# Ones multiplied until the first rows come, first weights split before the second turned pair, and other orders of the steps

## What is computed

```python
def first_block(x, p, ...):
    for i in range(DEPTH):                      # 2
        mix = mlstm_mixer(x, ...) if i < 1 else swa_sink_attention(x, ...)
        x = layer_norm(DEEPNORM_ALPHA * x + mix, mix_ln_g[i], mix_ln_b[i])
        x = layer_norm(DEEPNORM_ALPHA * x + squared_relu_mlp(x, ...), mlp_ln_g[i], mlp_ln_b[i])
        x = x + jax.nn.sigmoid(x @ ple_w_gate[i] + ple_b_gate[i]) * (p[i] @ ple_w_proj[i])
    return x

def second_block(x, p, ...):
    h = x + 0.5 * swiglu(rmsnorm(x, ffn1_norm), ...)
    u = rmsnorm(h, mix_norm) @ w_in
    h = h + mixed @ w_out                       # NSA (compressed, selected, window) and forgetting attention of u
    h = h + 0.5 * swiglu(rmsnorm(h, ffn2_norm), ...)
    gate = jax.nn.sigmoid(rmsnorm(h, ple_gate_norm) @ ple_w_gate)
    return h + gate * rmsnorm(p @ ple_w_proj, ple_norm)
```

## Time and profile before

| | us |
|---|---|
| median of 3 runs | 1218.65 |
| lowest and highest | 1217.24, 1219.37 |
| profiled execution, its time | 1217.5 |
| its span, first to last instruction | 1215.8 |
| TensorE busy | 1195.1 |
| VectorE busy | 744.2 |
| ScalarE busy | 619.4 |
| GpSimd busy | 42.6 |

### The profile page before, as it was taken

The page is one execution under the profiler, slowest core; times in us unless marked ns, Lnnn a source line. Parts: engine busy times, 40 slices in busy tenths (PEclk is TensorE's granted clock), DMA queues, the critical chain, the costliest instruction groups (busy, mean ns, idle before and its releaser), DMA issues.

```text
span 1215.8 us, 15115 instructions
## 1 busy us (share of the span) xinstructions
PE 1195.1 (98%) x5861; PEld 988.8 (81%) x5861; DVE 744.2 (61%) x983; ACT 619.4 (51%) x925; POOL 42.6 (4%) x61
## 2 busy tenths in 40 slices
PE   7999999999999999999999999999999999999998
PEld 6888788888778878888887888888878788888887
DVE  5759754556875675554596455547976465555446
ACT  5555444434465453443456344446886664444445
POOL 1000000000000000000001000001111010000000
PEclk9999999999999999999999999999999999999999
DMA  8555555555653456546555655554651336555550
GB/s 296 181 178 194 194 204 173 182 199 173 191 181 100 152 175 206 194 156 206 184 160 173 208 175 197 167 189 143 194 166 62 113 100 230 176 195 169 188 173 35
DMA packets 119959, 210.72 MB, mean 173 GB/s; under 512 B 8320, under 2 KB 67024, under 8 KB 119888
## 3 DMA queue, kind: packets, MB, share of 16 engines
q1 hardware_dynamic: 119344, 209.35, 52.2%
q10 hardware_dynamic: 544, 0.40, 0.1%
HBM read 208.68 MB, written 1.05 MB: 173 GB/s over the span
## 4 chain that ended last, share of the span: by engine, by line
PE 89%; DVE 7%; ACT 2%; issue 1%; POOL 0%; DMA 0%; DVEq 0%; ACTq 0%; POOLq 0%
PE psum L341 23%; PE psum L343 22%; PE psum L342 22%; PE psum L349 4%; PE psum L355 3%; PE psum L350 3%; PE psum L1364 2%; PE psum L1396 2%; PE psum L511 2%; DVE wl L324 2%; PE psum L1383 1%; PE psum L818 1%; PE psum L1370 0%; PE psum L1367 0%; ACT wh L314 0%
## 5 line engine op out<-in xcount | busy, mean ns | idle before, releaser
L293 DVE TENSOR_TENSOR wl<-ring,wh 128x2048 fp32r<-128x2048 f32 x131 | 300.0, 2292 | 269.2 <-ACT wh L284 269.0
L284 ACT ACTIVATE wh<-ring 128x2048 fp32r<-128x2048 f32 x131 | 250.7, 1916 | 219.1 <-PE psum L343 219.1
L341 PE MATMUL psum<-wh,xT_high 128*128 128x512 f32 (+4 forms) x816 | 319.8, 392 | 0.0
L343 PE MATMUL psum<-wh,xT_low 128*128 128x512 f32 (+4 forms) x816 | 312.7, 383 | 0.0
L342 PE MATMUL psum<-wl,xT_high 128*128 128x512 f32 (+4 forms) x816 | 312.0, 382 | 0.0
L341 PE MATMUL psum<-wh,hidT_high 128*128 128x512 f32 (+2 forms) x472 | 178.9, 380 | 0.2
L343 PEld LDWEIGHTS psum<-wh,xT_low 128*128 128x128 f32 x816 | 153.6, 188 | 30.0
L343 PE MATMUL psum<-wh,hidT_low 128*128 128x512 f32 (+2 forms) x472 | 177.9, 378 | 0.0
L342 PE MATMUL psum<-wl,hidT_high 128*128 128x512 f32 (+2 forms) x472 | 177.8, 378 | 0.0
L341 PEld LDWEIGHTS psum<-wh,xT_high 128*128 128x128 f32 x816 | 153.8, 188 | 28.7 <-issue 1.7
L342 PEld LDWEIGHTS psum<-wl,xT_high 128*128 128x128 f32 x816 | 153.9, 189 | 27.1
(11 more groups left out here) (301 smaller groups left out, 1311.2 us busy)
## 6 DMA issues: line engine op xcount, KB each, us to landing
ring<-in_mlp_w_up SPq DMA_DIRECT2D x32, 1024.0 KB, 5.3
ring<-in_mlp_w_down SPq DMA_DIRECT2D x32, 1024.0 KB, 4.9
ring<-in_ffn_wg SPq DMA_DIRECT2D x44, 512.0 KB, 4.0
ring<-in_ffn_wu SPq DMA_DIRECT2D x44, 512.0 KB, 5.0
ring<-in_ffn_wd SPq DMA_DIRECT2D x22, 1024.0 KB, 5.0
ring<-in_ple_w_gate SPq DMA_DIRECT2D x12, 1024.0 KB, 5.1
ring<-in_w_in SPq DMA_DIRECT2D x10, 1024.0 KB, 5.0
ring<-in_a_w_in SPq DMA_DIRECT2D x8, 1024.0 KB, 9.3
```

The source lines that it names most:

```text
L284: K.nc.scalar.activation(parts_of(K, n)[0][:, 0:w], K.ring[:, n % SLOTS, 0:w], ACT.Copy).then_inc(K.high_ready, 2)
L293: K.nc.vector.tensor_tensor(low[:, 0:w], K.ring[:, n % SLOTS, 0:w], high[:, 0:w].bitcast(F32), ALU.subtract).then_inc(K.low_ready, 2)
L341: nc.tensor.matmul(out, x[0], w[0], start=start, stop=False)
L343: return nc.tensor.matmul(out, x[1], w[0], start=False, stop=stop)
```

## The change

It has three parts.

1. VectorE sets the tile of ones first of all and signals it. TensorE waits for that signal and multiplies the tile with itself four times (float32, 128x256, into bank 0, which no one reads) ahead of its first step.
2. In the first stage's list "high 0, 0" and "low 0, 0" stand ahead of "xturn 1" for ScalarE and VectorE, and "high 0, 1" ahead of the first dense steps. Product 0's row tile 0 is done in pairs of k tiles: first high x high of both, as soon as the high weights are there, then low x high of both, then high x low, behind the wait for the low weights. The three products are the same, their order in the sum is not.
3. The lists of all tails and of the NSA stage have another order. No step is added or left out. The remaining 160 or so steps of the first stage's list keep their order.

The diff, cut: of part 3 it shows the list after the sinks, the one after the second embedding, and the stretch of the NSA list at the end of the dense work.

```diff
--- before.py
+++ after.py
@@ -925,27 +925,27 @@
     yield "stats", 0, 1
     yield "spread", 0
     yield "centre", 0, 0
+    yield "centre", 0, 1
     yield "normal", 0, 0
-    yield "centre", 0, 1
     yield "update", 1, 0
     yield "normal", 0, 1
+    yield "turn", 0, 0
     yield "last", 3, 1
-    yield "turn", 0, 0
     yield "turn", 0, 1
-    yield "high", 0, 0
+    yield "stats", 1, 0
+    yield "lead_low", 1, 0
     yield "update", 1, 1
     yield "low", 0, 0
-    yield "stats", 1, 0
     yield "stats", 1, 1
+    yield "lead_low", 1, 1
     yield "low", 0, 1
     yield "lead_high", 1, 0
     yield "lead_high", 1, 1
+    yield "high", 0, 0
     yield "high", 0, 1
     yield "lead", 0
     yield "lead", 1
-    yield "lead_low", 1, 0
     yield "spread", 1
-    yield "lead_low", 1, 1
     yield "centre", 1, 0
     yield "centre", 1, 1
     yield "normal", 1, 0
...
@@ -1112,15 +1112,17 @@
     yield "square", 0, 0
     yield "lead_high", 0, 1
     yield "lead_low", 0, 0
+    yield "gate", 0, 0
     yield "turn", 0, 0
-    yield "gate", 0, 0
+    yield "sigmoid", 0
     yield "lead_high", 1, 0
     yield "lead_high", 1, 1
     yield "high", 0, 0
-    yield "sigmoid", 0
     yield "high", 0, 1
+    yield "square", 0, 1
+    yield "sigmoid", 1
+    yield "logit", 0
     yield "lead_low", 0, 1
-    yield "logit", 0
     yield "gated", 0
     yield "gate", 0, 1
     yield "gate", 1, 0
@@ -1129,8 +1131,6 @@
     yield "lead_low", 1, 0
     yield "low", 0, 0
     yield "logit", 1
-    yield "sigmoid", 1
-    yield "square", 0, 1
     yield "low", 0, 1
     yield "gated", 1
     yield "lead_low", 1, 1
...
@@ -2152,343 +2152,343 @@
...
+        yield "take", 5, 0
+        yield "keep", 21
         yield "scores", 22
         yield "low", 18, 1
         yield "shares", 4
-        yield "take", 5, 0
         yield "high", 19, 0
+        yield "dense", 5, 1, 1, range(2)
+        yield "dense", 5, 1, 1, range(2, 4)
         yield "norm", 4
         yield "take", 5, 1
-        yield "dense", 5, 1, 1, range(2)
-        yield "keep", 21
-        yield "dense", 5, 1, 1, range(2, 4)
+        yield "turn", 20
+        yield "values", 19
+        yield "zturn", 0, 0
+        yield "high", 19, 1
+        yield "tiles", 4
+        yield "turn", 21
         yield "group", 4
-        yield "turn", 20
-        yield "zturn", 0, 0
-        yield "values", 19
-        yield "high", 19, 1
-        yield "turn", 21
-        yield "values", 20
-        yield "tiles", 4
         yield "low", 19, 0
-        yield "low", 19, 1
         yield "tiles", 5
         yield "tiles", 6
-        yield "values", 21
         yield "tiles", 7
         yield "scores", 23
+        yield "values", 20
+        yield "values", 21
         yield "keep", 22
         yield "turn", 22
-        yield "keep", 23
+        yield "low", 19, 1
         yield "scores", 24
         yield "out", 0, 0, 0
...
@@ -3027,12 +3027,12 @@
     def steps():
 
         yield "xturn", 0
-        yield "xturn", 1
         yield "high", 0, 0
         yield "low", 0, 0
+        yield "xturn", 1
+        yield "high", 0, 1
         yield "dense", 0, 0, 0, range(2)
         yield "dense", 0, 0, 1, range(2)
-        yield "high", 0, 1
         yield "low", 0, 1
         yield "xturn", 2
         yield "xturn", 3
@@ -3227,6 +3227,9 @@
 
     @block.tensor
     def _(pe):
+        pe.wait_ge(K.ones_ready, 1)
+        for i in range(4):
+            nc.tensor.matmul(K.psum[:, 0, 0:SEQ], K.ones[:, 0:P], K.ones[:, :], start=True, stop=True)
         for step, *args in steps():
             if step == "dense":
                 c, half, t, ks = args
@@ -3239,18 +3242,24 @@
                         pe.wait_ge((K.act_took if t == 0 else K.dve_took).sem, c - 1)
                 w = [joined(x, 4, width) for x in parts_of(K, n)]
                 out_c = K.psum[:, bank(c, t), 0:width]
+                if c == 0 and t == 0:
+                    xs = lambda k, part: K.xT[part][:, 4 * half + k, 0:P]
+                    for a in ks[::2]:
+                        pe.wait_ge(K.input_high.sem, (4 * half + a) // 2 + 1)
+                        pe.wait_ge(K.high_ready, 2 * n + 1 + a // 2)
+                        for k in (a, a + 1):
+                            nc.tensor.matmul(out_c, xs(k, 0), w[0][:, k, :], start=half == 0 and k == 0, stop=False)
+                        pe.wait_ge(K.input_low.sem, (4 * half + a) // 2 + 1)
+                        for k in (a, a + 1):
+                            nc.tensor.matmul(out_c, xs(k, 1), w[0][:, k, :], start=False, stop=False)
+                        weights_here(K, pe, n, a // 2)
+                        for k in (a, a + 1):
+                            mm = nc.tensor.matmul(out_c, xs(k, 0), w[1][:, k, :], start=False, stop=half == 1 and k == 3)
+                    if half == 1:
+                        mm.then_inc(K.filled.sem, 1)
+                    continue
                 for k in ks:
                     kk = 4 * half + k
-                    if c == 0 and t == 0:
-                        if k % 2 == 0:
-                            pe.wait_ge(K.input_high.sem, kk // 2 + 1)
-                            weights_here(K, pe, n, k // 2)
-                        product_high(K, out_c, stationary(K.xT)(kk, t), [x[:, k, :] for x in w], kk == 0)
-                        if k % 2 == 1:
-                            pe.wait_ge(K.input_low.sem, kk // 2 + 1)
-                            product_low(K, out_c, stationary(K.xT)(kk - 1, t), [x[:, k - 1, :] for x in w], False)
-                            mm = product_low(K, out_c, stationary(K.xT)(kk, t), [x[:, k, :] for x in w], kk == KT - 1)
-                        continue
                     if k % 2 == 0:
                         weights_here(K, pe, n, k // 2)
                     mm = product(K, K.psum[:, bank(c, t), 0:width], stationary(K.xT)(kk, t),
@@ -3468,10 +3477,11 @@
     def _(dve):
         ch = Chain(dve, K.dve_step)
         S, G = K.mstat, K.gates
+        nc.vector.memset(K.ones[:, :], 1.0).then_inc(K.ones_ready, 1)
         for ap, value in [(K.ident[:, :], 0.0), (K.sel[:, :, :], 0.0), (K.causal[:, :], 0.0),
                           (K.window[:, :], 0.0), (K.cmp_mask[:, :, :], 0.0), (K.cmp_keep[:, :, :], 1.0)]:
             nc.vector.memset(ap, value).then_inc(K.zeroed, 1)
-        for ap, value in [(K.ones[:, :], 1.0), (K.fox_bias[:, :], 0.0), (K.minus_half[:, :], -0.5),
+        for ap, value in [(K.fox_bias[:, :], 0.0), (K.minus_half[:, :], -0.5),
                           (K.v_ext[:, :, :, M_DV:M_DV + 1], 1.0), (K.cmp_v[:, :, :], 0.0),
                           (K.half_rows[0:HD, 0:1], 1.0), (K.half_rows[HD:P, 0:1], 0.0),
                           (K.half_rows[0:HD, 1:2], 0.0), (K.half_rows[HD:P, 1:2], 1.0)]:
@@ -4096,6 +4106,7 @@
         K.first_loaded = sem("first_loaded")
         K.small_loaded = sem("small_loaded")
         K.zeroed = sem("zeroed")
+        K.ones_ready = sem("ones_ready")
         K.masked = sem("masked")
         K.p_loaded = sem("p_loaded")
         K.stored = sem("stored")
```

More of the change, by code:

```diff
@@ L2269, in steps @@
-        yield "silu", 0
-        yield "dense", 3, 1, 0, range(2)
-        yield "high", 13, 1
-        yield "dense", 3, 1, 0, range(2, 4)
-        yield "gate", 2
-        yield "low", 13, 0
+        yield "keep", 4
+        yield "cw1", 1, 1, range(4, 8)
+        yield "high", 12, 0
+        yield "gate", 2
+        yield "high", 12, 1
+        yield "low", 12, 1
+        yield "high", 13, 0
+        yield "high", 13, 1
+        yield "turn", 4
+        yield "dense", 3, 1, 0, range(2)
+        yield "silu", 0
```

359 lines of the change are left out of this document (178 added, 181 removed).

## The result

The changed kernel took 1214.95 us (median of 7 executions, 1213.33 to 1215.91), the kernel before in the same rounds 1218.65 us. The ratio is 0.9969, with a 95% interval of 0.9959 to 0.998: 3.7 us faster, where 3.3 us were forecast. The profiled execution took 1214.99 us with a span of 1213.3 us, 2.5 us under the 1215.8 us of the profile before. So the two profiles show only part of what the medians show: the kernel before was profiled in an execution 1.15 us under its median, the changed one in an execution at its median. The gain read from rows (2.5 us) is not the gain of the medians (3.7 us).

The account below looks back on a forecast made before the run. TensorE is busy 98% of 1215.8 us, so gains lie in its 20 us of waits and slow-clock stretches. 2.4 + 0.6 + 0.3 = 3.3 us off the median of 1218.65 gave 1215.4 us, range 1212.8 to 1217.8.

Parts of the forecast that it names:

- The fillers and the splits: Start: high clock by the first dense matmul, up to 1.9 us; with earlier splits TensorE 4.2 us ahead after load 1.
- What is late next: Gate transposes: VectorE's copy of product 0, behind "bias", limits the start's lead to 2.4 us (bounds 1.9 to 2.8).
- The lists: Start: the small lists (gains, biases, positions) that "bias" waits for, forecast to land at 23.57 again.
- The rival that was given 0.07: Start: TensorE's new stand of 1.95 us makes the clock fall, half of 4.06 us lost: 1217.4 us, chance 0.07.
- the 2.54 us wait: Start, ahead of 9.21: the clock was low after TensorE's wait, but nothing shows that it had been high.
- the slower rival: Start: small lists share DMA time with loads 5 and 6 and land at 28.2: 1220.0 us, chance 0.05.
- Second embedding: Logit 0 after one lead half, sigmoid ahead of ScalarE's splits, VectorE's 0.98 us idle filled: 0.6 us (0 to 1.0).
- Sinks: After the sinks: "centre 0 1" fills VectorE's 0.50 us wait for GpSimd's rstd: 0.3 us (0 to 0.5).
- Other seams and NSA: Remaining seams 0 (-0.2 to +0.2 each); reordered NSA steps 0 (-1.0 to +1.0), twenty of 341 steps traced.
- too little for the lists: Reordered step lists behind the start: 0.9 us forecast, 0.6 at the second embedding and 0.3 after the sinks.
- too much for the start: Lead gained by the gate transposes, the largest term: 2.4 us forecast.

Follow-up runs that it names:

- the lists alone: The kernel before with all the changed step lists, the NSA stage's among them, and its old start: 1217.86 us (11 executions), ratio 0.9988.
- four kernels: Changed lists with old start, 1217.86 us; changed kernel without fillers, 1213.77; that with product 0's copy ahead of bias, 1215.09; kernel before with new NSA order, 1217.51.
- the first half of the sinks' order alone: The kernel before with "centre 0 1" ahead of "normal 0 0" and "turn 0 0" ahead of "last 3 1": one execution, 1220.0 us.
- its start alone: The kernel before with parts 1 and 2 of the change, all step lists after the start as before: 1216.11 us (11 executions), ratio 0.998.
- the second half of the sinks' order: The kernel before with "stats 1 0" and both "lead_low 1" steps ahead, "high 0 0" behind "lead_high 1 1": one execution, lead gained 0.0 us, no time given.

## Why the forecast was right, and where two errors cancelled

The time (1214.95 for 1215.4 us), its sign and the range held. The terms did not all hold.

**The fillers and the splits: right.** Four matmuls of ones ended at the first rows, the high clock held at the first dense matmul, that one came at 7.42 (7.2 forecast), the end of load 2, counted by the starts of the matmuls as in the forecast, at 22.6 (22.4). The 0.2 us are the first weight half: it landed only at 6.42, and ScalarE waited 0.36 us for it, which the forecast's chain didn't have.

**What is late next: right, by name and by mechanism.** The copy of product 0 behind "bias" was the cap. Moving that one step gave 2.1 us more than the changed kernel without a fall. The forecast's words that the fillers alone decide nothing also held, and for the reason given. The lists landed at 24.02 instead of 23.57; the profiles of the other kernels have VectorE's step for them at 23.49 to 24.80. So the stand ended at a lead of 1.82 us, just under the term's lower bound of 1.9: 0.45 us of the difference to 2.4 are the later lists.

**The rival that was given 0.07 is what happened in about half of the executions.** "The new stand of 1.95 us makes the clock fall" was named and priced nearly right (2.0 us; measured 1.6). Its chance was the error. The step that failed is the sentence that the low clock behind the 2.54 us wait proves nothing because the clock may not have been high: true, but it was then used as if it spoke against a fall. A row that is silent should have left the chance open. The Trainium skill, TensorE: Matmul & The Clock Gate, "Part 1: The HAM clock gate", says that the clock is set by how busy the array has been recently, and that the number of slow matmuls at the start of one kernel differs from run to run. The runs agree with the first: filling the stands took the falls away. For the second they show more than the start: three of seven executions of the changed kernel had no fall, and the others had.

**The range's other side.** The lists did not land 2 us later than before in any profile (the latest was 24.80 against the 26.9 from which that rival decides), so the slower rival had no case. That later loads start behind the lists, as the Trainium skill, DMA: Bandwidth & Descriptors, "Queues, rings and completion order", has it, is in line with this but not shown by it.

**Second embedding: size right (0.67 for 0.6), the wait that goes was another.** The forecast followed the 0.57 us wait at 647.65. It is still there in the changed kernel, at 645.57. What went is the wait for "gated 0" at the transposes, in the kernel before:

```profile
641.17 0.66 PE L818 MATMUL psum<-ident,x 128*128 128x128 f32 x4 [0.47 <-DVE x L3833]
```

The part that VectorE's idle 0.98 us would be filled and gated 0 come 0.9 us sooner was right: it has no such idle time in the changed kernel, and gated 0 starts at 637.24 for 639.70, 2.5 us sooner, of which 1.4 are the lead brought along.

**Sinks: 0.6 for 0.3, and the reason wrong.** Filling VectorE's 0.50 us wait for GpSimd was to be the gain. That half of the edit alone loses 0.36 us. The step that failed is that VectorE's chain behind "turn 0 0" has no gap to lose: TensorE's last product, now behind the new stand, opens one of 0.87 us. The forecast also never looked at TensorE's waits of 0.79 and 0.18 us for the weights at 430.62 and 431.96, which are what the second half of the edit removes.

**Other seams and NSA: 0.56 and 0.4 us for 0 and 0.** Each was judged by the one wait in the table of waits, if at all, and put at nothing. For the list after the first embedding the forecast gives no reason, and its 0.3 us lie outside the +0.2 allowed to each seam. The NSA gain lies within the bounds given (+-1.0), but the forecast named no new stand there, and the new order joins two waits (0.43 and 0.82 us) into the one of 1.83 us behind which the clock can fall. These traces were not taken apart further.

In sum 1.4 us too little for the lists and, in the executions in which the clock fell, 2.2 us too much for the start; in those in which it held, 0.6 us too much (1.8 for 2.4). Where the clock holds, the whole gain is 4.1 us (1217.5 us, the profiled execution before, to 1213.4 us) and not 3.3. In the two profiles it is 2.5 us; that the medians are 3.7 us apart comes from the 1.15 us by which the median before lay above its profile, while the changed kernel's did not. The median forecast was met because errors of opposite sign, and the choice of execution that each median happens to be, cancelled, and that is luck, not a right sum.

## What to carry to other kernels

When an edit makes TensorE arrive earlier, ask at once what it will wait for, who stands ahead of that in the other engine's queue, and whether a wait that is not needed (here for biases that the copy doesn't read) can be moved behind it: that one line was worth 2.1 us. A new stand of TensorE costs its own length and puts what follows at risk of half the clock; filling it with products that nobody reads cost nothing measurable here (1211.35 against 1211.25 us) and, where all of them were filled, took the long executions away. And where executions scatter in groups, compare group with group and read leads at the same instruction in both traces, since a median only says which group was more frequent.

## What was unexpected of the hardware

Stands of 1.83, 2.13 and 2.50 us ahead of an otherwise busy stretch were enough for TensorE's granted clock to go to 0.50, for 3.4 us at the start and 6.8 us near 945 us, and this in some executions and not in others of the same kernel: behind the 2.1 us stand probably in three of seven (one is profiled), and with the 1.83 us stand of the NSA stage left empty in about half of the executions of the lists alone (six of 11) and 15 of 36 over four kernels. Even these lengths are no lower limit. One fall, at 8.0 us, followed a wait of only 1.67 us, shortly after the clock had risen, and in the first half of the sinks' order alone one of 3.4 us followed waits of 0.43 and 0.81 us, which three other profiled kernels have too, with no fall behind them (the kernel before, its start alone, and the second half of the sinks' order). The falls cost 1.3 to 2.7 us each. In four profiles TensorE spent the stands on products of ones (2.3 us ahead of the gate transposes, 1.5 us ahead of the first weights, 1.9 us in the NSA stage, twice, and 0.6 and 1.0 us there in the old order), and none of the four has a fall. Why the NSA fall lasts 3.4 us in one kernel and 6.8 us in another was not tested.
